# Sixteen of 48 modulation tiles of the first layer: from TensorE sums beside the attention projections to VectorE dot products beside the output projection

## The chip, the core and the metric

The kernel runs on one core of one Trainium2 chip, and nothing else runs on it. The metric is the device time of one execution in microseconds (us). PE is TensorE, PEld its weight loads, DVE VectorE, ACT ScalarE, POOL GpSimd, SP SyncE, which here only issues DMAs. A matmul of four bytes per element is done here as three passes over a rounded high part and a remainder of weight and data, so every weight unit (512 KB) is split on its way: ACT copies its high part (tile `WH`), DVE subtracts it from the raw unit (`WL`).

## What is computed

Two trunks of two layers each run one behind the other. Every layer begins with a vector of modulations, a matrix product of a conditioning vector with a weight of 1024 x 6144; the vector exists for the image (`c`) and for the context (`c_ctx`):

```python
c_act = jax.nn.silu(c); cc_act = jax.nn.silu(c_ctx)
mx = jnp.split(c_act @ ada_w[i] + ada_b[i], 6, axis=-1)
mc = jnp.split(cc_act @ ada_w[i] + ada_b[i], 6, axis=-1)
h_x = modulate(rms_norm(x, norm1_g[i]), mx[0], mx[1])
...
x = x + mx[2] * out_x                       # attention and its output projection
x = x + mx[5] * swiglu(modulate(rms_norm(x, norm2_g[i]), mx[3], mx[4]), ...)
```

The 6144 modulations of a layer are 48 tiles of 128. Tiles 0 to 15 (shift and scale of the first norm) are wanted at once, tiles 16 to 23 (`mx[2]`) at the output projection, tiles 32 to 39 (scale of the second norm) right behind it, tiles 24 to 31 (its shift) with them, and tiles 40 to 47 (`mx[5]`) only in the feed-forward.

## The kernel before

Each engine has its own program, written out by hand, and they meet at semaphores (`on(name, event)` is the value to wait for). Everything of a layer stays in SBUF: 768 columns of tokens (512 image, 256 context), 8 tiles of 128 features.

**Modulations of layer 0.** They are made on TensorE in 12 parts of 512 columns. `ada_sum` (line 761) waits for the two halves of a part (1 MB each, tiles `aV` and `aAR`, issued by SP) and does 16 matmuls of 32 x 512; ACT copies the sum (`ada_copy`, line 1251, `aKF`); `ada_turn` (line 769) turns it by 4 matmuls with a selector, and `ada_finish` adds the bias. (The profile counts a four-byte matmul as more than one record, so a group of four is seen as x8 or x16.) Four parts are made before and in the first norm. The other eight stand one behind each product of the projections of keys and queries: product `u + p`, p from 2 to 9, then the sum of part 4 + QK[p]; its turn stands within the product after it. Beside each product also runs the norm of its head pair: PE sums squares (`square_sum`, line 919), ACT takes the root (line 1256), DVE refines it and turns the pair by its position (`newton` at 1909, then 2372, `stream_shuffle`, sines and cosines). ACT waits within this for `q_normed` (line 2372's result), and the last square sum (of p = 9) stands 18 matmuls into the products for the values (`product_rows`, line 747), where PE waits for `q_squared` of p = 9 and the root of p = 8.

**Modulations of the later layers.** They are made on DVE, in the feed-forward of the layer before: a tile of transposed weights (128 x 1024, 512 KB, `AT`, two buffers, issued by POOL) times the conditioning vector spread over all partitions (`CB`, on which ACT has done Silu, line 1457), with the sum along the row as accumulator (`scalar_tensor_tensor`, line 1895), once for each of the two vectors.

**The output projection.** Eight products `u + n` of 24 x 2 matmuls (line 638; the last two, in `product_tail`, line 682, go by groups, first both over the context, then both over the image). Products alternate between two PSUM tiles, so product n + 2 waits for `x_out` n. On DVE, `project` does for n from 0 to 5: wait for product n, `X += PS * MOD` in two instructions (line 2108), then the low part of the weight of product n + 3 (`refill`, line 1862). Behind n = 1 it does `log_sigmoid`, some twenty small instructions on 8 columns (lines 2732 to 2742). ACT does the high part of the same weight and the square of the new `X` (line 1261), POOL adds the squares up (line 2780: 768 columns, both inputs in SBUF). The second norm begins when the first tail tiles are taken (line 2090). SP issues the weight of unit u + n + 3 as soon as its buffer is free, one queue, in order.

Of the kernel before, what the change touches and what calls it, by code (L numbers as in the profile page):

```python
# [6 lines left out]
ALU = mybir.AluOpType  # L7
# [7 lines left out]
P = 128  # L15
# [15 lines left out]
RING = 6  # L31
Q = 384
NV = 6 * D // P
NA = 6 * D // 512
A0 = 4
EPS = 1e-6
UNIT = KT * P
# [2 lines left out]
U0 = -(S + P)  # L40
NU = L + S - U0
NB = 5 * P + 1
FIRST_PARTS = [0, 2, 1, *range(3, NA)]
FIRST_ADA = (30720, 38912, 49152, 57344, 65536, 73728, 87584, 95776)


# [163 lines left out]
class Memory:  # L210
# [118 lines left out]
    def attention(self):  # L329
        t = self.tile  # L330
        self.aQ = t("aQ", [P, 8, T])
        self.aK = t("aK", [P, 4, 2, T], F32R)
        self.aV = t("aV", [P, 8, L])
        QS0 = t("aQS0", [P, 16, P], F32R)
        top = self.top
        self.aRAW = [t(f"aR{i}", [P, T]) for i in range(2)]
        self.aSQ = t("aSQ", [P, T])
        self.aRI = t("aRI", [P, T])
        self.aT2 = t("aT2", [P, S])
        self.aKF = t("aKF", [P, T])  # L340
        self.aCOS = t("aCOS", [P, S])
        self.aSIN = t("aSIN", [P, S])
        self.aBD = t("aBD", [P, P])
        self.aQG = t("aQG", [P, 2])
        self.aAR = t("aAR", [P, 4, 512])
        self.top = top
        self.aQS = [QS0, t("aQS1", [P, 16, P], F32R)]
        self.aP = [t(f"aP{i}", [P, NB]) for i in range(4)]
        self.aPT = [t(f"aPT{i}", [P, 5 * P]) for i in range(4)]
        self.aID = t("aID", [P, P])  # L350
        self.aMK = t("aMK", [P, 5 * P])
        self.aSK = t("aSK", [P, 16])
        self.aNM = t("aNM", [P, 16])
        self.aRSM = t("aRSM", [P, 16])

    def retention(self):
        t = self.tile
# [264 lines left out]
def tensor_program(PE, M, on, FIRST):  # L622
# [288 lines left out]
    def attention():  # L911
        u = FIRST["qkv"]
        buf = (flat(M.aV, 0, 8).rearrange("p (a n) -> p a n", a=4), M.aAR)

        def square_sum(p):
            PE.wait_ge(*on("q_squared", QK[p]))
            PE.wait_ge(*on("rms", ("q", QK[p - 1])) if p else on("table", "attention"))
            for a, b, _ in ALL:
                mm = PE.matmul(PS[2][:, a:b], M.aBD[:, :], M.aSQ[:, a:b], start=True, stop=True)
            mm.then_inc(*on.up("q_square_sum", QK[p]))  # L920

        def beside(p, at, squares_at, turn_at):

            if at == squares_at and p != 1:
                square_sum(p)
            if at == turn_at and p > 1:
                ada_turn(0, A0 + QK[p], M.aKF)

        product_pair(u, PS, ALL, ("h_lo", "0a", 0), beside_first, amid_first)
        for p in range(2, 10):  # L930
            last = p - 1 if p > 2 else 0
            product(u + p, PS[p % 2], (HH, HL), KT, ALL, ("q_squared", QK[p - 2]), None,
                    lambda k: beside(last, k, 3 if p == 3 else 2, 5))
            if p == 2:
                square_sum(1)
            ada_sum(0, A0 + QK[p], buf, (0, A0 + QK[p] - 1))
        for half in range(2):
            product_rows(u + 10 + half, 4, 4 * half, L, range(6), lambda m: v_place(PS, m), half == 0, half == 1, None, True,
                         (lambda m: ("v_rows", m // 2) if m in (1, 3) else None) if half else None,
                         None if half else lambda at: beside(9, at, 6, 14))  # L940

        PE.wait_ge(*on("aV", 1))
        for step in range(HEADS + LAG + 2):
            i = step
            if i < HEADS:
                b, n = i // 16, i % 16
                kh, ps = M.aK[:, 2 * (n // 8) + n % 2, :, :], PS[n % 2]
                if n == 0:
                    PE.wait_ge(*on("q_stacked", (b, 1)))
                if i == 1:  # L950
                    PE.wait_ge(*on("aV", 2))
                if i > 1:
                    PE.wait_ge(*on("a_max", i - 2))
                for at, k, count in runs(keys(b)):
                    for f in range(2):
                        mm = PE.matmul(ps[:, at * P:(at + count) * P], M.aQS[b % 2][:, n, :], kh[:, f, k * P:(k + count) * P],
                                       start=f == 0, stop=f == 1)
                mm.then_inc(*on.up("a_scores", i))
# [12 lines left out]
            if i >= 0 and i % 2 == 0:
                b, t = i // 16, i % 16 // 2
                out = bank(PS, 6 + t // 4)[:, t % 4 * P:(t % 4 + 1) * P]
                PE.wait_ge(*on("a_turned", i + 1))
                if i == 0:
                    PE.wait_ge(*on("step", ("mod", 0, 2)))
                if t % 4 == 0 and b:
                    PE.wait_ge(*on("o_lo", (b - 1, t // 4)))
                tiles = keys(b)
                for k, kt in enumerate(tiles):  # L980
                    for g in range(2):
                        v0 = (2 * (t // 4) + g) * 64
                        mm = PE.matmul(out[64 * g:64 * g + 64, :], M.aV[:, kt, v0:v0 + 64], M.aPT[(i + g) % 4][:, k * P:(k + 1) * P],
                                       start=(k == 0), stop=(k == len(tiles) - 1))
                mm.then_inc(*on.up("a_values", i // 2))
# [239 lines left out]
def scalar_program(AC, M, on, FIRST, W):  # L1225
# [305 lines left out]
    def attention():  # L1531
# [13 lines left out]
        for p, n in enumerate(QK):  # L1545
# [7 lines left out]
            AC.activation(M.aSQ[:, :], PS[p % 2][:, 0:T], SQUARE).then_inc(*on.up("q_squared", n))  # L1553
            if p:
                refill(u + p + 2)
            if n < 8:
                ada_copy(0, A0 + n, M.aKF[:, 0:512])
            rsqrt(("q", n), M.aRI[:, :], PS[2][:, 0:T], M.aSQ[:, :], ("q_square_sum", n))
            AC.wait_ge(*on("q_normed", n))
            if n in (6, 7):  # L1560
# [290 lines left out]
def vector_program(VE, M, on, FIRST, W):  # L1851
# [14 lines left out]
        ins.then_inc(*on.up("step", event))  # L1866
        VE.wait_ge(*on("step", event))

    def ada_finish(l, part, v0, v1):
        VE.wait_ge(*on("ada_turned", (l, v1 // 4 - 1)))  # L1870
        tr = M.tr.rearrange("p (v j) -> p v j", j=2)
        for j in range(2):
            i = VE.tensor_tensor(MOD[:, l, v0:v1, j], tr[:, v0:v1, j], M.ADB[:, l, v0:v1], ALU.add)
        step(i, ("mod", l, part))
        scales(l, part, v0, v1)

    def scales(l, part, v0, v1):
        for which in range(2):
# [224 lines left out]
    def project(l, segs):  # L2103
        u = FIRST["out", l]
        for n in range(KT - 2):
            VE.wait_ge(*on("product", u + n))
            for a, b, j in segs:
                i = VE.scalar_tensor_tensor(X[:, n, a:b], PS[n % 2][:, a:b], MOD[:, l, 16 + n, j:j + 1], X[:, n, a:b],
                                            ALU.mult, ALU.add)
            i.then_inc(*on.up("x_out", (l, n)))  # L2110
            refill(u + n + 2)
            if l == 0 and n == 1:
                log_sigmoid()

    def turned(l, n):

# [233 lines left out]
    def attention():  # L2350
# [44 lines left out]
        VE.wait_ge(*on("rope", QK[-1]))  # L2395
        for g in range(2):
            stack(0, g)
        ada_finish(0, 2, 4 * A0, NV)
        for v in range(2):
            refill(u + 12 + v)  # L2400
        VE.wait_ge(*on("rope_ctx", QK[-1]))
# [365 lines left out]
def pool_program(PO, M, on, dram):  # L2767
# [15 lines left out]
    def modulation(f, n):  # L2783
# [4 lines left out]
        if n > 1:  # L2788
            PO.wait_ge(*on("ada_taken", order[n - 2]))
        l, v = order[n]  # L2790
        PO.dma_start(M.AT[n % 2][:, :], dram["adat"][l - 1, v]).then_inc(*on.up(f"mod_load{n % 2}", (l, v), 16))  # L2791

    def feed_forward(l):

# [27 lines left out]
    for t, name in ((M.CIN, "cin"), (M.SEL, "sel"), (M.LG, "decay"), (M.ADB, "adb"), (M.GN, "gn"), (M.FG, "finalg"), (M.CW, "ffnconv")):  # L2822
# [2 lines left out]
        src = dram[name]  # L2825
        PO.dma_start(ap, src if len(src.shape) == 2 else src.rearrange("p a b c -> p (a b c)")).then_inc(
            *on.up("c_load" if name in ("cin", "sel") else "small", 0, 16))
    attention()
    PO.wait_ge(*on("o_lo", (5, 1)))
    squares("0b", T)  # L2830
# [23 lines left out]
def sync_program(SP, M, on, FIRST, W, dram, out):  # L2854
# [39 lines left out]
    u = FIRST["qkv"]  # L2894
    buf = (M.aV[:, :, :].rearrange("p (a b) n -> p a (b n)", b=2), M.aAR[:, :, :])
    for n in range(12):
        part = {0: 0}.get(n, n - 2 if 2 < n < 10 else None)
        if part is not None:
            for half in range(2):
                ada(0, A0 + part, half, buf, (0, A0 + part - 1))  # L2900
# [7 lines left out]
    SP.dma_start(M.aID[:, :], dram["ident"]).then_inc(*on.up("aID", 0, 16))  # L2908

    u = FIRST["out", 0]  # L2910
    for n in range(KT):
        load(u + n + 3)
    SP.wait_ge(*on("o_lo", (5, 1)))
    feed_forward(0)

    u = FIRST["ret"]
# [60 lines left out]
def layout(x):  # L2977
# [20 lines left out]
            sel[32 * q + j, j] = 1  # L2998
    d["sel"] = sel
    w = np.concatenate([a["ada_w"], a["w_ada_2"]], 0)  # L3000
    d["ada"] = w[0].reshape(2, 4, P, 12, 512).transpose(3, 0, 2, 1, 4)[FIRST_PARTS].reshape(24, P, 4, 512)
    d["adat"] = w[1:].transpose(0, 2, 1).reshape(3, NV, P, D)
    cb = np.stack([np.stack([a["c"][0], a["c_ctx"]], 0), np.stack([a["c_2"][0], a["c_ctx_2"]], 0)], 0)
    d["cb"] = np.broadcast_to(cb.reshape(2, 1, 2 * D), (2, P, 2 * D))

# [117 lines left out]
```

## Time and profile before

| | |
|---|---|
| Median of 3 runs | 3359.18 us (3356.56 to 3360.82) |
| The profiled execution | 3358.63 us, span of its core 3357.3 us |
| PE busy | 3243.3 us, 97% of the span |
| PE weight loads | 2767.6 us, 82% |
| DVE busy | 2150.5 us, 64% |
| ACT busy | 1389.9 us, 41% |
| POOL busy | 221.0 us, 7% |
| Mean granted PE clock | 0.991 of full speed |
| HBM read | 329.37 MB, 99 GB/s over the span |

The shares are means over stages that differ: in the projections of keys and queries PE has no gap at all, in the attention PE, DVE and ACT take turns, and in the output projection DVE works less than a third of the time. A change that moves work from one stage and engine to another is read from those two stages.

### The profile page before, as it was taken

What the parts mean: (1) busy time and instruction counts of PE and PEld (TensorE: products, weight loads), DVE (VectorE), ACT (ScalarE), POOL (GpSimd) and SP (SyncE); (2) the same over time, 40 slices, a digit from 0 to 9 for tenths busy, and PEclk for the clock granted to TensorE, in tenths of its full rate; (3) what the DMA queues carried; (4) which work ended last, traced back from release to release, by engine and by line L of the source; (5) the groups of instructions that cost most, each with busy time, mean ns of one, the idle gap of its engine ahead of it and who ended that gap; (6) DMA issues with size and microseconds to landing.
All of it is one profiled execution on the core that took longest, in us unless ns stands there. A gap on an engine that the chain in (4) does not pass through costs nothing. (4 is left out here: it accounts for less than half of the span.)

```text
span 3357.3 us, 45065 instructions
## 1 busy us (share of the span) xinstructions
PE 3243.3 (97%) x17830; PEld 2767.6 (82%) x17830; DVE 2150.5 (64%) x3560; ACT 1389.9 (41%) x2242; POOL 221.0 (7%) x336
## 2 busy tenths in 40 slices
PE   7998999999999999999999999999999999999998
PEld 5787789999978888878878886889999987688887
DVE  5678477888665545558788466476777865654444
ACT  5478353333444324342223345353333444542332
POOL 0001100000000000003111000100000010010001
PEclk9999999999999999999999999999999999999999
DMA  6500124444221221226664211113333231122232
GB/s 242 201 23 1 38 74 128 144 132 140 91 93 46 101 78 47 88 76 200 204 200 167 85 45 51 38 67 116 113 104 110 83 103 57 44 88 94 94 101 76
DMA packets 98689, 334.39 MB, mean 100 GB/s; under 512 B 11872, under 2 KB 16768, under 8 KB 95024
## 3 DMA queue, kind: packets, MB, share of 16 engines
q1 hardware_dynamic: 77072, 252.63, 22.4%
q0 software_dynamic: 21408, 78.88, 7.4%
q8 instruction: 142, 2.33, 0.3%
q14 instruction: 67, 0.55, 0.1%
HBM read 329.37 MB, written 2.10 MB: 99 GB/s over the span
## 5 line engine op out<-in xcount | busy, mean ns | idle before, releaser
L1245 ACT ACTIVATE WH<-WR 128x1024 fp32r<-128x1024 f32 (+3 forms) x516 | 443.1, 863 | 916.0 <-PE PS L638 679.5
L1862 DVE TENSOR_TENSOR WL<-WR,WH 128x1024 fp32r<-128x1024 f32 (+3 forms) x516 | 507.9, 986 | 449.1 <-ACT WH L1245 447.9
L638 PE MATMUL PS<-HH,WH 128*128 128x512 f32 x1608 | 544.2, 373 | 8.7 <-DVE WK L2295 3.4
L638 PE MATMUL PS<-HH,WL 128*128 128x512 f32 x1608 | 539.7, 370 | 0.0
L638 PE MATMUL PS<-HL,WH 128*128 128x512 f32 x1608 | 539.2, 369 | 0.0
L638 PE MATMUL PS<-D,WH 128*128 128x512 f32 x1648 | 420.9, 361 | 1.5 <-DVE D L2319 1.4
L638 PEld LDWEIGHTS PS<-HH,WH 128*128 128x128 f32 x1608 | 280.6, 189 | 69.6 <-issue 9.9
L638 PEld LDWEIGHTS PS<-HL,WH 128*128 128x128 f32 x1608 | 279.4, 189 | 52.8 <-issue 1.0
L638 PEld LDWEIGHTS PS<-HH,WL 128*128 128x128 f32 x1608 | 279.7, 189 | 52.2
L638 PEld LDWEIGHTS PS<-D,WH 128*128 128x128 f32 x1648 | 275.7, 188 | 52.6 <-DVE D L2319 3.2
L638 PE MATMUL PS<-D,WL 128*128 128x512 f32 (+1 forms) x824 | 257.3, 360 | 0.0
L2073 DVE SCALAR_TENSOR_TENSOR X<-PS,MOD,X 128x512 f32<-128x512 f32 x198 | 121.2, 644 | 168.7 <-PE PS L638 137.0
L850 PE MATMUL PS<-HH,WH 128*128 128x384 f32 x608 | 204.2, 336 | 4.6 <-DVE WK L2172 4.6
L850 PE MATMUL PS<-HL,WH 128*128 128x384 f32 x608 | 203.7, 335 | 0.0
L850 PE MATMUL PS<-HH,WL 128*128 128x384 f32 x608 | 203.3, 334 | 0.0
L1895 DVE SCALAR_TENSOR_TENSOR AT<-AT,CB 128x1024 f32<-128x1024 f32 x144 | 177.7, 1234 | 8.1 <-ACT CB L1457 6.2
L850 PE MATMUL PS<-XH,WH 128*128 128x384 f32 x456 | 155.1, 340 | 7.3 <-ACT WK L1414 7.3
L638 PEld LDWEIGHTS PS<-D,WL 128*128 128x128 f32 x824 | 138.1, 188 | 25.0
L850 PE MATMUL PS<-XH,WL 128*128 128x384 f32 x456 | 154.5, 339 | 0.0
L850 PE MATMUL PS<-XL,WH 128*128 128x384 f32 x456 | 154.5, 339 | 0.0
L747 PE MATMUL PS<-WH,HH 128*128 128x256 f32 (+1 forms) x416 | 140.5, 338 | 5.1 <-DVE HL L1979 5.1
L2791 POOL DMA_DIRECT2D AT<-in_adat x144 | 76.5, 531 | 995.9 <-DVE AT L1895 980.1
(377 smaller groups left out, 6042.5 us busy)
## 6 DMA issues: line engine op xcount, KB each, us to landing
WR<-in_win SPq DMA_DIRECT2D x176, 512.0 KB, 3.5
AT<-in_adat POOLq DMA_DIRECT2D x144, 512.0 KB, 3.9
WR<-in_wret SPq DMA_DIRECT2D x64, 512.0 KB, 3.7
WR<-in_zin SPq DMA_DIRECT2D x36, 512.0 KB, 3.5
WR<-in_wdn SPq DMA_DIRECT2D x32, 448.0 KB, 3.4
WR<-in_wdn SPq DMA_DIRECT2D x48, 256.0 KB, 2.7
WR<-in_wdn SPq DMA_DIRECT2D x32, 320.0 KB, 3.0
AR<-in_ada SPq DMA_DIRECT2D x8, 1024.0 KB, 19.1
```

Source lines behind the costliest of these rows:

```text
L638: mm = PE.matmul(dst[:, a:b], w(u)[:, k * P:(k + 1) * P], h[:, k, a:b], start=(k == 0 and i == 0), stop=(k == nk - 1 and i == 2))
L747: mm = PE.matmul(dst(m), h[:, k0 + k, m * P:(m + 1) * P], w(u)[:, k * width:(k + 1) * width], start=(first and k == 0 and i == 0 and not ( ...
L850: mm = PE.matmul(dst, w(key)[:, k * P:(k + 1) * P], h[:, k, :], start=(k == 0 and n == 0 and i in (1, 2, 7)), stop=(k == 3 and n == 2), sk ...
L1245: AC.activation(M.hi(u), M.raw(u), COPY).then_inc(*on.up("w_hi", u))
L1862: VE.tensor_tensor(M.lo(u), M.raw(u), M.hi(u).bitcast(F32), ALU.subtract).then_inc(*on.up("w_lo", u))
L1895: i = VE.scalar_tensor_tensor((AT if j == len(cols) - 1 else PS[3])[:, :], AT[:, :], 1.0, M.CB[:, j, :], ALU.mult, ALU.mult, accum_out=MOD ...
L2073: i = VE.scalar_tensor_tensor(X[:, m, a:b], src[:, a:b], MOD[:, l, 40 + m, j:j + 1], X[:, m, a:b], ALU.mult, ALU.add)
L2791: PO.dma_start(M.AT[n % 2][:, :], dram["adat"][l - 1, v]).then_inc(*on.up(f"mod_load{n % 2}", (l, v), 16))
```

## The change

It takes tiles 24 to 31 and 40 to 47 of layer 0 from TensorE. The parts shrink from 12 to 8 (`NA` = 8), so the sums and turns behind products 6, 7, 8 and 9 go, with their loads and copies. The 16 tiles are made as in later layers, by `first_dots` on DVE: before it waits for product n of the output projection it makes 3 tiles for n = 0 to 3 and 2 for n = 4 and 5 (`FIRST_AT`), each with two dot products of 128 x 1024 against a new tile `CB0` (1 MB, loaded by POOL's queue in the first norm; ACT does Silu on it at p = 8, between the copies of the pair and the root). SP loads the tiles into `AT`, two buffers, in its queue of weights; tile i waits until tile i - 2 is taken. None can be loaded before the attention ends, as `AT` lies where the attention's tiles are, and SP now waits there (`o_lo`) after one weight where it had issued those it could. A sum with the bias (`first_bias`) follows behind n = 5.

```diff
-NA = 6 * D // 512
+FIRST_PARTS = [0, 2, 1, 3, 4, 5, 8, 9]
+FIRST_DOTS = [*range(24, 32), *range(40, 48)]
+FIRST_AT = (0, 3, 6, 9, 12, 14, 16, 16, 16)
+NA = len(FIRST_PARTS)
...
+        self.aDT = t("aDT", [P, D])
+        self.top = top
...
+        self.CB0 = t("CB0", [P, 2, D])
...
-            if at == turn_at and p > 1:
+            if at == turn_at and p > 1 and A0 + QK[p] < NA:
                 ada_turn(0, A0 + QK[p], M.aKF)
...
-            ada_sum(0, A0 + QK[p], buf, (0, A0 + QK[p] - 1))
+            if A0 + QK[p] < NA:
+                ada_sum(0, A0 + QK[p], buf, (0, A0 + QK[p] - 1))
...
-            if n < 8:
+            if A0 + n < NA:
                 ada_copy(0, A0 + n, M.aKF[:, 0:512])
+            if p == 8:
+                AC.wait_ge(*on("cb_load", 0))
+                AC.activation(M.CB0[:, :, :], M.CB0[:, :, :], ACT.Silu).then_inc(*on.up("cb", 0))
             rsqrt(("q", n), M.aRI[:, :], PS[2][:, 0:T], M.aSQ[:, :], ("q_square_sum", n))
...
+    def first_dots(at):
+
+        for n in range(FIRST_AT[at], FIRST_AT[at + 1]):
+            v = FIRST_DOTS[n]
+            if n == 0:
+                VE.wait_ge(*on("cb", 0))
+            VE.wait_ge(*on(f"ada_load{6 + n % 2}", ("dot", v)))
+            if n:
+                VE.wait_ge(*on("ada_taken", (0, FIRST_DOTS[n - 1])))
+            for j in range(2):
+                i = VE.scalar_tensor_tensor((M.AT[n % 2] if j else M.aDT)[:, :], M.AT[n % 2][:, :], 1.0, M.CB0[:, j, :],
+                                            ALU.mult, ALU.mult, accum_out=MOD[:, 0, v, j:j + 1])
+            i.then_inc(*on.up("ada_taken", (0, v)))
+
+    def first_bias():
+        VE.wait_ge(*on("ada_taken", (0, FIRST_DOTS[-1])))
+        for v0, v1 in ((24, 32), (40, 48)):
+            for j in range(2):
+                i = VE.tensor_tensor(MOD[:, 0, v0:v1, j], MOD[:, 0, v0:v1, j], M.ADB[:, 0, v0:v1], ALU.add)
+        step(i, ("mod", 0, 3))
...
         for n in range(KT - 2):
+            if l == 0:
+                first_dots(n)
             VE.wait_ge(*on("product", u + n))
...
+            if l == 0 and n == KT - 3:
+                first_bias()
...
+    PO.wait_ge(*on("ada_sum", (0, A0 - 1, 1)))
+    PO.dma_start(flat(M.CB0, 0, 2), dram["cb"][0]).then_inc(*on.up("cb_load", 0, 16))
...
     u = FIRST["out", 0]
+    load(u + 3)
+    SP.wait_ge(*on("o_lo", (5, 1)))
     for n in range(KT):
-        load(u + n + 3)
-    SP.wait_ge(*on("o_lo", (5, 1)))
+        if n:
+            load(u + n + 3)
+        for i, v in list(enumerate(FIRST_DOTS))[FIRST_AT[n]:FIRST_AT[n + 1]]:
+            if i > 1:
+                SP.wait_ge(*on("ada_taken", (0, FIRST_DOTS[i - 2])))
+            SP.dma_start(M.AT[i % 2][:, :], dram["adat"][0, v]).then_inc(*on.up(f"ada_load{6 + i % 2}", ("dot", v), 16))
```

## Rows read from the trace of the kernel before

**Rows 1.** Stages: us, busy time per engine, PE clock, DMA share, GB/s.
```profile
94.86:145.49 50.63, 50.63 (x305) 37.60 (x304) 36.20 (x53) 26.82 (x41) 0.00 (x0) 1.00 0.55 208
...
353.15:405.66 52.51, 52.51 (x288) 45.53 (x289) 17.10 (x37) 9.56 (x10) 10.53 (x6) 0.97 0.17 51
```

**Rows 2.** Timeline of PE, projections of queries: start, us, line, tile, count.
```profile
145.05 0.51 PE L638 MATMUL PS<-HH,WL 128*128 128x512 f32 x2
...
145.49 1.06 PE L761 MATMUL PS<-aV,CAC 128*32 128x512 f32 x8
...
147.34 0.62 PE L638 MATMUL PS<-HH,WH 128*128 128x512 f32 x2
...
154.03 0.95 PE L769 MATMUL PS<-SEL,aKF 128*128 128x2 f32 x8
...
154.84 0.59 PE L638 MATMUL PS<-HH,WH 128*128 128x512 f32 x2
...
158.13 1.07 PE L761 MATMUL PS<-aV,CAC 128*32 128x512 f32 x8
...
162.24 1.02 PE L919 MATMUL PS<-aSQ,aBD 128*128 128x512 f32 x2
```

**Rows 3.** Timeline of ACT, the same stretch.
```profile
147.00 1.06 ACT L1245 ACTIVATE WH<-WR 128x1024 fp32r<-128x1024 f32 x1
...
151.05 0.90 ACT L1256 ACTIVATE aRI<-PS,EPSC 128x768 f32<-128x768 f32 x1 [2.51 <-PE PS L919]
```

**Rows 4.** Instructions of line 1457: ns min/median/max, first and last start.
```profile
L1457 ACT ACTIVATE CB<-CB x2: 1919/1919/1919, 496.5 to 2262.6; 128x2048 f32<-128x2048 f32 x2
```

**Rows 5.** Timeline of ACT behind the output projection.
```profile
412.57 1.28 ACT L1256 ACT_TABLE_LOAD   x1
```

**Rows 6.** Timeline of DVE, projections of queries and values.
```profile
152.87 0.96 DVE L1909 SCALAR_TENSOR_TENSOR aSQ<-PS,aSQ 128x768 f32<-128x768 f32 x1 [3.55 <-ACT aSQ L1258]
...
154.85 1.02 DVE L2372 SCALAR_TENSOR_TENSOR aR<-aR,aQG,aRI 128x768 f32<-128x768 f32 x1
...
180.85 1.23 DVE L1862 TENSOR_TENSOR WL<-WR,WH 128x1024 fp32r<-128x1024 f32 x1 [3.94 <-ACT WH L1245]
```

**Rows 7.** Instructions of line 1895, the dot products of later layers.
```profile
L1895 DVE SCALAR_TENSOR_TENSOR AT<-AT,CB x144: 1210/1219/1749, 498.5 to 2668.6; 128x1024 f32<-128x1024 f32 x144
```

**Rows 8.** Timeline of DVE, the output projection.
```profile
363.47 1.14 DVE L2108 SCALAR_TENSOR_TENSOR X<-PS,MOD,X 128x512 f32<-128x512 f32 x2 [10.37 <-PE PS L638]
...
364.62 1.23 DVE L1862 TENSOR_TENSOR WL<-WR,WH 128x1024 fp32r<-128x1024 f32 x1
...
374.24 1.82 DVE L2732 TENSOR_SCALAR MOD<-MOD 128x8 f32<-128x8 f32 x1
...
380.50 1.14 DVE L2108 SCALAR_TENSOR_TENSOR X<-PS,MOD,X 128x512 f32<-128x512 f32 x2
...
408.74 0.48 DVE L2090 SCALAR_TENSOR_TENSOR X<-PS,MOD,X 128x256 f32<-128x256 f32 x1 [0.50 <-PE PS L682]
```

**Rows 9.** DMA issues of the output projection's weights: count, KB, us to landing.
```profile
WR<-in_wo SPq DMA_DIRECT2D x8, 512.0 KB, 3.8
```

**Rows 10.** Timeline of POOL, the output projection.
```profile
365.58 1.97 POOL L2780 TENSOR_TENSOR WK<-WK,WK 128x768 f32<-128x768 f32 x1 [11.68 <-ACT WK L1261]
...
374.05 1.98 POOL L2780 TENSOR_TENSOR WK<-WK,WK 128x768 f32<-128x768 f32 x1 [6.50 <-ACT WK L1261]
```

**Rows 11.** Timeline of DVE, dot products beside POOL.
```profile
1544.34 1.65 DVE L1895 SCALAR_TENSOR_TENSOR PS<-AT,CB 128x1024 f32<-128x1024 f32 x1
```

**Rows 12.** Timeline of POOL, the same stretch.
```profile
1544.15 0.74 POOL L2809 TENSOR_TENSOR WK<-X 128x256 f32<-128x256 f32 x1
```

**Rows 13.** Timeline of PE after a wait in the feed-forward.
```profile
504.38 0.66 PE L850 MATMUL PS<-XH,WH 128*128 128x384 f32 x1 [3.81 <-ACT WK L1414]
```

**Rows 14.** Stage behind that wait; columns as in rows 1.
```profile
504.38:507.40 3.02, 3.02 (x10) 3.02 (x10) 2.68 (x6) 2.34 (x5) 0.00 (x0) 0.50 0.82 283
```

More of the change, by code:

```diff
@@ L42 @@
 NB = 5 * P + 1
-FIRST_PARTS = [0, 2, 1, *range(3, NA)]
 FIRST_ADA = (30720, 38912, 49152, 57344, 65536, 73728, 87584, 95776)
@@ L1867, in step, with ada_finish @@
         VE.wait_ge(*on("step", event))
-    def ada_finish(l, part, v0, v1):
-        VE.wait_ge(*on("ada_turned", (l, v1 // 4 - 1)))
+    def ada_finish(l, part, pieces):
+        VE.wait_ge(*on("ada_turned", (l, NA - 1)))
         tr = M.tr.rearrange("p (v j) -> p v j", j=2)
-        for j in range(2):
-            i = VE.tensor_tensor(MOD[:, l, v0:v1, j], tr[:, v0:v1, j], M.ADB[:, l, v0:v1], ALU.add)
+        for v0, v1 in pieces:
+            for j in range(2):
+                i = VE.tensor_tensor(MOD[:, l, v0:v1, j], tr[:, v0:v1, j], M.ADB[:, l, v0:v1], ALU.add)
         step(i, ("mod", l, part))
-        scales(l, part, v0, v1)
+        scales(l, part, pieces[0][0], pieces[-1][1])
+    def first_dots(at):
[13 more added lines that the diff above has]
+        for v0, v1 in ((24, 32), (40, 48)):
+            for j in range(2):
+                i = VE.tensor_tensor(MOD[:, 0, v0:v1, j], MOD[:, 0, v0:v1, j], M.ADB[:, 0, v0:v1], ALU.add)
+        step(i, ("mod", 0, 3))
     def scales(l, part, v0, v1):
@@ L2397, in attention @@
             stack(0, g)
-        ada_finish(0, 2, 4 * A0, NV)
+        ada_finish(0, 2, ((16, 24), (32, 40)))
         for v in range(2):
@@ L2790, in modulation @@
         l, v = order[n]
[L2791 removed]
+        PO.dma_start(M.AT[n % 2][:, :], dram["adat"][l, v]).then_inc(*on.up(f"mod_load{n % 2}", (l, v), 16))
     def feed_forward(l):
@@ L2896, in sync_program @@
     for n in range(12):
-        part = {0: 0}.get(n, n - 2 if 2 < n < 10 else None)
+        part = {0: 0}.get(n, n - 2 if 2 < n < 3 + NA - A0 - 1 else None)
         if part is not None:
@@ L3000, in layout @@
     w = np.concatenate([a["ada_w"], a["w_ada_2"]], 0)
-    d["ada"] = w[0].reshape(2, 4, P, 12, 512).transpose(3, 0, 2, 1, 4)[FIRST_PARTS].reshape(24, P, 4, 512)
-    d["adat"] = w[1:].transpose(0, 2, 1).reshape(3, NV, P, D)
+    d["ada"] = w[0].reshape(2, 4, P, 12, 512).transpose(3, 0, 2, 1, 4)[FIRST_PARTS].reshape(2 * NA, P, 4, 512)
+    d["adat"] = w.transpose(0, 2, 1).reshape(4, NV, P, D)
     cb = np.stack([np.stack([a["c"][0], a["c_ctx"]], 0), np.stack([a["c_2"][0], a["c_ctx_2"]], 0)], 0)
```

## The prediction

> **What bounds the kernel.** I read first the table of stages, for the two stages the change touches. Between 94.86 and 145.49 us, four periods of the query projections, PE is busy for all of the 50.63 us at full clock; between 353.15 and 405.66, the first six products of the output projection, again for all of the 52.51, while DVE works 17.10 [rows 1]. In both stages the end is set by the sum of what PE does; in the second DVE has 35 us free. Then I read the timelines of PE, ACT and DVE of one period of the first stage, for what leaves it and what waits behind it, and those of DVE and POOL in the second, for what fits into it. The chain of waits, followed back from the end, does not reach these stages and says nothing here.
>
> **What is removed.** One period of PE, from sum to sum, is 158.13 - 145.49 = 12.64 us. The 16 matmuls of a sum stand between the last pair of a product (145.05 plus the 0.35 that pairs are apart) and the next product at 147.34: 1.94. The turn takes 154.84 - 154.03 = 0.81. Each new start costs some 0.08 more, so a sum with its turn is worth 2.9, and a period without them 9.74 [rows 2]. Four go: 11.6 us. Loads of 2 MB a period and the copy by ACT were hidden and are worth nothing. Is there another chain that keeps the period at 12.6? ACT starts the root of p = 8 at 151.05, 5.65 after the product's end at 145.40, because the square sum stands behind the modulation sum [rows 3]; it moves up by 1.94. DVE starts the refinement 1.82 later and is done with the pair some 6 us after that, which is 11.3 after the product's end; the next pair's root then starts at 9.74 + 3.7. DVE and ACT stay ahead by about a microsecond, and the period follows PE.
>
> **What is added there.** The Silu of `CB0` on ACT at p = 8. It has 2048 columns, 1.92 us [rows 4], and changes the table before and after it, 1.28 each [rows 5]: 4.48 us. The refill of ACT ends at 147.95 [rows 3], so the root starts at 152.5 in place of 149.1. The result for which ACT waits next (line 2372) ends 154.85 + 1.02 = 155.87, that is 4.8 after the start of the root [rows 6]: now 157.3. Behind it ACT copies 0.4, and only then takes the raw copy and the square of p = 9, 1.5 together: 159.2. PE comes to that square sum 2.25 into the products for the values (162.24 against 158.13 + 1.86) [rows 2], which is 145.40 + 9.74 + 2.25 = 157.4. It waits 1.8 us. Before the attention DVE stood idle for 3.94 us until these products were done [rows 6]; its pair of p = 9 now ends later against them by about a microsecond, which that idle time covers. The load of `CB0` meets only loads of parts and weights that are wanted later. Gain of this stage: 11.6 - 1.8 = 9.8 us; at most 11.6 (no wait), at least 8 (if the chain of DVE holds the three short periods up by 0.6 each).
>
> **What is added in the output projection.** I count DVE's time from the start of product 0 (353.15). The dots are 32 at 1.22 each with little overlap [rows 7]: 2.4 us a tile, 38.4 in all; 2.3 if they overlap fully, 2.5 with the wait for the tile before. An update of `X` with its refill takes from 363.47 to 365.8: 2.3, and `log_sigmoid` from 374.24 to the next update at 380.50: 6.2 [rows 8]. Four more costs:
>
> First, tile 0 can't be loaded before the attention ends. The nearest row is a unit of the same 512 KB on the same queue, 3.8 us from issue to landing [rows 9], with 0.2 for the semaphore 4.0.
>
> Second, with two buffers tile i is issued when tile i - 2 is taken, and the dots of tile i - 1 (2.4) cover only part of 3.8 + 0.3. In each group of three the third tile waits 1.6 us; the first two have the update, or more, as cover. Four groups: 6.4. For groups of two nothing.
>
> Third, POOL. Its square sum starts 0.97 after an update is done (365.58 against 363.47 + 1.14), waits for the end of the refill and runs 1.78 to 367.55 [rows 8, 10]. Today nothing follows the refill but an idle stretch. The one exception is `log_sigmoid`: its first instruction on 8 columns takes 1.82 us and ends 376.06, as POOL's sum does at 376.03 [rows 8, 10]. A dot beside a short POOL instruction until 1544.89 started at 1544.34 and took 1.65, not 1.22 [rows 11, 12]: held for 0.4, then run at its own speed. Now a dot stands behind the refill for n = 0, 2, 3 and 4, and is held about 1.6 each time: 6.4. If instead the two shared the bandwidth, the dot would take 1.35 times as long (1.65 / 1.22) for 1.9 us: 0.5 each, 2.0 in all. The 1.82 is nearest to the first reading, and I take it.
>
> The Trainium skill bears on this (SBUF — State Buffer, Who interferes with whom): DVE with two inputs in SBUF and a GpSimd instruction that reads SBUF exclude each other for the whole instruction, and the one issued second waits. By that rule the four holds are 6.4, by the sharing that I weighed it against 2.0; the trace agrees with the rule on the 1.82 us, and update instructions with one input in PSUM would not be held.
>
> Fourth, SP's queue: the weights of n = 1 to 5 now stand between tiles. Each lands many microseconds before ACT wants it; nothing.
>
> The sum until the update of n = 5 is done: 4.0 + 38.4 + 6.4 + 6.4 + five updates with refill 11.5 + 6.2 + the last update 1.1 = 74.0 us. PE was there at 408.74 - 0.2 - 353.15 = 55.4: the second tail tile needs that update, and the first tail tile over the context was then done [rows 8]. So PE falls back 18.6. It does so in pieces: product 4 waits for the update of n = 2, which ends near 43.5 where PE is free at 35.6; product 5 waits for n = 3, near 56 against 52; the second tail tile waits near 6 us. All of them lie in DVE's one sequence, so the first waits don't add to the last.
>
> Then the tail. The bias (four small adds and a semaphore, 0.7) is held by POOL's sum of n = 5, 1.6, and stands ahead of the first tail tile's update. The mean of the context is then ready about 1 us late for PE. Or, PE's clock: after a wait of 3.81 us its next matmuls of 384 columns took 0.66 and on [rows 13], with the granted clock at 0.50 for 3.0 us, 1.2 in place of 2.4 GHz [rows 14]; it lost 1.4 us. Behind a wait of 6 us I expect the same. The two overlap: 1.0 us for both together, at most 2.5. The clock that falls in product 4 is absorbed, as PE waits for DVE again behind it. Loss of this stage: 19.6 us; at least 12.6 (third cost at 2.0, tail at nothing, tiles at 2.3), at most 25 (landings of 5 us, tiles of 2.5).
>
> What follows, the second norm and the feed-forward, is the same work and moves as a whole. Net: 19.6 - 9.8 = +9.8, against the profiled 3358.63 us: 3368.4. That execution lies 0.55 under the median of the three; a measured median would be 3369. I take 3368.5 us.
>
> **The rivals.** All times against 3358.6. Less than 0.2% (6.7 us) can hardly be told from no change, so the bounds are 3351.9 and 3365.3.
>
> *The port is shared, not locked, and the tail hides its wait.* Loss 19.6 - 4.4 - 1.0 = 14.2, net +4.4: 3363.0, no difference. For it: POOL's instruction lengths vary, and some of a hold may fall into a wait for a tile. Against it: the 1.82 us for 8 columns.
>
> *The other side: the free 35 us of DVE are enough.* With no waits for tiles, no holds and tiles of 2.3, the sum is 59.6, the loss 4.2, and with the whole 11.6 of the first stage the kernel is 7.4 faster: 3351.2. The mechanism is a tile's cost, its waits included: to pass 0.2% it must be under 2.23 us where the gain is 9.8 (the loss may be 3.1, so DVE's sequence 58.5, less 22.8 for all that is not a tile, by 16), and under 2.34 where it is 11.6. The dots alone take 2.3 to 2.4. What speaks for it is only the busy share of DVE.
>
> *Landings are slow.* SP's queue has weights between the tiles; if a tile behind a weight lands after 6 us and not 3.8, each of the four waits and the first grow by 2.2: +11, net +20: 3379. For it: two transfers share the engines. Against: the two need only a small share of the DMA engines in this stage (0.17 now, under 0.5 then).
>
> *The first stage keeps its period*, because the norm chain of ACT and DVE sets it: gain 3 in place of 9.8, 3375. Against it: PE has no gap at all there and waits for neither.
>
> **Chances.** The forecast 0.56, ports shared or milder 0.25, DVE has room 0.04, slow landings 0.09, first stage keeps its period 0.06. So faster 0.04, same 0.27 (the second case, and little of the forecast's lower edge), slower 0.69. The forecast alone spans 3365 to 3373 (tile 2.3 to 2.5, 1.5 for landings, 1.5 for the clock). The range for 8 in 10 takes in most of the milder case and the upper edge: 3362 to 3375.
>
> **What the profile would show.** Right: periods of 9.7 us behind product 6, a PE wait near 1.8 in the products for the values, DVE without a gap from 357 on (all less 9.8) but for four waits for DMA of 1.6; a dot of 2.8 us behind the refills of n = 0, 2, 3 and 4; PE waits of about 8, 3 and 6 us, named DVE `X`. Wrong: dots of 1.65 there (shared), the wait of products 4 and 5 missing (DVE has room), waits for DMA of 4 (slow landings), or periods still over 11.

## The result, and the profile after

The changed kernel took 3367.22 us (median of 8 runs, 3365.36 to 3371.38), the kernel before 3356.39 us beside it (8 runs, 3353.96 to 3360.82). The ratio is 1.0031, with a 95% interval of 1.0021 to 1.0040: 7 to 13 us slower (10.8 by the medians), where 9.8 was forecast, and inside the range of 3362 to 3375. The profiled execution took 3365.97 us, with a span of 3364.5.

The page's busy times show where work went: PE 9.6 us less than before, DVE 45.9 more.

```profile
PE 3233.7 (96%) x17734; PEld 2764.5 (82%) x17734; DVE 2196.4 (65%) x3630; ACT 1391.8 (41%) x2241; POOL 221.2 (7%) x337
```

**First stage.** The timeline of ACT after the change, at p = 8:

```profile
139.72 0.81 ACT L1556 ACTIVATE aR<-PS 128x768 f32<-128x768 f32 x1 [1.09 <-PE PS L643]
140.43 0.81 ACT L1559 ACTIVATE aSQ<-PS 128x768 f32<-128x768 f32 x1
141.12 1.06 ACT L1251 ACTIVATE WH<-WR 128x1024 fp32r<-128x1024 f32 x1
142.20 1.28 ACT L1566 ACT_TABLE_LOAD   x1
143.49 1.92 ACT L1566 ACTIVATE CB<-CB 128x2048 f32<-128x2048 f32 x1
145.43 1.28 ACT L1262 ACT_TABLE_LOAD   x1
146.72 0.90 ACT L1262 ACTIVATE aRI<-PS,EPSC 128x768 f32<-128x768 f32 x1
```

The Silu and its two table loads stand between the refill (ends 142.18) and the root (146.72): 4.5 us. The raw copy before this one starts at 129.95, so a period without a sum is 9.77 us, against 12.64 [rows 2]. In PE's timeline the price of the Silu is one wait, in the products for the values:

```profile
151.33 0.28 PE L752 MATMUL PS<-WH,HL 128*128 128x256 f32 x1
153.44 1.56 PE L924 MATMUL PS<-aSQ,aBD 128*128 128x512 f32 x4 [1.83 <-ACT aSQ L1559]
```

From the first square sum of the queries to the first scores of the attention, 123.98 us became 114.50: 9.5 gained. The attention behind it takes the same time (171.31 before, 171.43 after).

**Output projection.** DVE's timeline after the change: the three tiles before the update of n = 0, what stands behind the refills of n = 0, 1 and 4, and the end:

```profile
347.31 1.23 DVE L1897 SCALAR_TENSOR_TENSOR aDT<-AT,CB 128x1024 f32<-128x1024 f32 x1 [3.65 <-DMA AT<-in_adat]
348.46 1.22 DVE L1897 SCALAR_TENSOR_TENSOR AT<-AT,CB 128x1024 f32<-128x1024 f32 x1
...
349.79 1.23 DVE L1897 SCALAR_TENSOR_TENSOR aDT<-AT,CB 128x1024 f32<-128x1024 f32 x1
...
353.08 1.23 DVE L1897 SCALAR_TENSOR_TENSOR aDT<-AT,CB 128x1024 f32<-128x1024 f32 x1 [0.91 <-DMA AT<-in_adat]
...
355.37 1.14 DVE L2141 SCALAR_TENSOR_TENSOR X<-PS,MOD,X 128x512 f32<-128x512 f32 x2
356.43 1.22 DVE L1871 TENSOR_TENSOR WL<-WR,WH 128x1024 fp32r<-128x1024 f32 x1
357.56 2.88 DVE L1897 SCALAR_TENSOR_TENSOR aDT<-AT,CB 128x1024 f32<-128x1024 f32 x1
...
369.65 1.82 DVE L2767 TENSOR_SCALAR MOD<-MOD 128x8 f32<-128x8 f32 x1
...
406.88 2.88 DVE L1897 SCALAR_TENSOR_TENSOR aDT<-AT,CB 128x1024 f32<-128x1024 f32 x1
...
413.31 1.14 DVE L2141 SCALAR_TENSOR_TENSOR X<-PS,MOD,X 128x512 f32<-128x512 f32 x2
...
415.50 2.03 DVE L1905 TENSOR_TENSOR MOD<-MOD,ADB 128x8 f32<-128x8 f32 x4
```

Two tiles of a group start 2.48 apart (347.31, 349.79). The third waits 0.91 for its transfer (1.09, 1.02 and 1.12 in the next groups). The dot behind a refill takes 2.88 and not 1.22, and the small adds of the bias take 2.03. POOL's timeline beside it:

```profile
357.48 1.87 POOL L2815 TENSOR_TENSOR WK<-WK,WK 128x768 f32<-128x768 f32 x1 [13.03 <-ACT WK L1267]
...
406.79 1.89 POOL L2815 TENSOR_TENSOR WK<-WK,WK 128x768 f32<-128x768 f32 x1 [6.74 <-ACT WK L1267]
415.40 1.87 POOL L2815 TENSOR_TENSOR WK<-WK,WK 128x768 f32<-128x768 f32 x1 [6.73 <-ACT WK L1267]
```

POOL's sum ends at 359.35 and the dot that started at 357.56 at 360.44, 1.1 later: it stood until POOL was done and then ran at its own speed. PE's timeline shows where it waits for the updates:

```profile
385.27 0.98 PE L643 MATMUL PS<-HH,WH 128*128 128x512 f32 x2 [6.56 <-DVE X L2141]
397.36 0.58 PE L643 MATMUL PS<-HH,WH 128*128 128x512 f32 x2 [0.69 <-DVE X L2141]
414.60 0.55 PE L687 MATMUL PS<-HH,WH 128*128 128x256 f32 x1 [5.51 <-DVE X L2141]
```

Behind the first and the last of these waits PE works at half its clock. The windows of these stretches after the change (granted clock third from the end):

```profile
385.27:391.00 5.73, 5.73 (x18) 4.87 (x19) 5.63 (x6) 1.68 (x2) 1.87 (x1) 0.50 0.26 87
414.60:418.80 4.20, 4.20 (x20) 4.20 (x21) 3.41 (x6) 1.15 (x2) 2.09 (x2) 0.53 0.36 127
```

The stage by windows, first before and then after: from product 0 to the second tail tile, and from there to the first product of the feed-forward.

```profile
353.15:408.55 55.40, 55.40 (x313) 48.42 (x314) 19.46 (x40) 11.47 (x12) 11.11 (x7) 0.97 0.16 48
408.55:445.57 37.02, 33.79 (x178) 27.95 (x176) 25.22 (x43) 21.24 (x37) 3.42 (x3) 1.00 0.09 29
```
```profile
343.71:414.60 70.89, 58.13 (x313) 50.41 (x313) 61.78 (x104) 10.40 (x12) 10.11 (x6) 0.89 0.49 171
414.60:453.43 38.83, 35.57 (x176) 29.74 (x176) 28.15 (x48) 21.98 (x38) 3.89 (x3) 0.95 0.08 28
```

DVE works 61.78 of 70.89 us, where it worked 19.46 of 55.40: it has become the bound. The stage lost 15.5 us, and the norm behind it 1.8: 17.3. The 1.8 is PE's clock: behind the second tail tile PE is busy for 35.57 us in place of 33.79, and its gaps are the same (3.26 and 3.23). The bias, which POOL holds for 1.65 us, shows in no gap of PE. Less the 9.5 of the first stage that is 7.8 us by landmarks (starts of chosen instructions, the same in every profile), and the two profiled spans differ by 7.2. How far a profile can be trusted here: the start-up before the first square sum of the queries ended anywhere from 57.7 to 59.8 us in the eleven profiles of this study.

### The profile page after: what moved, and what is told of

Same layout as the page of the kernel before. It is cut to its first block and busy times, and to the rows that moved or that the text cites. A ratio compares the mean times of both kernels' runs of the same rounds, so it can differ in the third digit from the quotient of the medians.

```text
span 3364.5 us, 44958 instructions
## 1 busy us (share of the span) xinstructions
PE 3233.7 (96%) x17734; PEld 2764.5 (82%) x17734; DVE 2196.4 (65%) x3630; ACT 1391.8 (41%) x2241; POOL 221.2 (7%) x337
```

## The experiments

Times below are medians in us; a ratio is against the kernel before, in runs beside the kernel's own. There it took 3357.67 (30 runs) beside the first stage alone, the short sums, the four buffers and the later Silu, 3357.93 (19) beside the row in PSUM and the last three kernels, and 3356.67 (15) beside the later logarithm. Three landmarks are read from each profile: first square sum of the queries to first scores (123.98 before, 114.50 after), product 0 to the end of the update of n = 5 (53.86, 70.74), and product 0 to the feed-forward's first product (92.42, 109.72).

### first_stage_alone: what the first stage gives by itself

The four sums stay away, and the 16 tiles are made nowhere (only the bias is left of them).

```diff
-            if l == 0:
-                first_dots(n)
...
-        for i, v in list(enumerate(FIRST_DOTS))[FIRST_AT[n]:FIRST_AT[n + 1]]:
...
-            SP.dma_start(M.AT[i % 2][:, :], dram["adat"][0, v])
```

> The changed kernel without its dot products and without the loads of their tiles (the sixteen tiles are left out, only a bias is written); the sums on TensorE are gone and the Silu on ScalarE stays. It measures the gain of the first stage by itself. My theory: the output projection starts 9.4 us earlier, as in the profile of the changed kernel, nothing is lost behind it, and the kernel is 9.4 us faster than before (ratio 0.9972). Rival, that the work removed from TensorE was partly hidden and the 9.4 us are given back elsewhere: 3 us or less. Rival, that the loss of the change lies in later stages and not in the output projection: then it is still slower than before.

Measured: 3347.21 (3344.70 to 3351.52), ratio 0.9971 (0.9961 to 0.9982). Landmarks 114.50, 53.86 and 92.43: the first is that of the changed kernel, the other two those of the kernel before to 0.01 us. So the change is the sum of two independent parts, and the first is worth 9.5 us with its Silu in place.

### short_pool_sums: POOL's sums made short

The sum of squares of n = 0 to 5 goes over 8 columns in place of 768; most of that sum is left out.

```diff
+            if tag == "0b" and b - a == n:
+                b = a + 8
```

> The changed kernel, with the six sums of squares that GpSimd does beside the output projection cut from 768 columns to 8 (most of these sums of squares is left out). It tests whether the dot products that took 2.9 us are held by GpSimd. Port held for a whole instruction: the four dots behind the refills take 1.3 in place of 2.9 us, the first instruction of the logarithm 0.2 in place of 1.8, the bias loses 1.6 too; VectorE's sequence to the last update shrinks by 8.2 us from 70.7 to about 62.5, the second tail tile waits not at all or 1 us, and the kernel is 7 to 9 us faster than the changed one, about 2 to 3 above the one before less: ratio to before near 1.0005. Bandwidth shared: the dots take 1.2 to 1.5 and the gain is near 2 us. If the 2.9 us come from something else (the DMA that writes the next tile): unchanged, ratio 1.003.

Measured: 3357.16 (3355.43 to 3361.26), ratio 1.0002 (0.9993 to 1.0010). The update of n = 5 ends at 62.40, 8.3 earlier: five holds of 1.65, four of dots and one of `log_sigmoid`. The timeline of DVE in this kernel, behind the refills of n = 0 and 1:

```profile
358.56 1.22 DVE L1897 SCALAR_TENSOR_TENSOR aDT<-AT,CB 128x1024 f32<-128x1024 f32 x1
...
368.94 0.17 DVE L2767 TENSOR_SCALAR MOD<-MOD 128x8 f32<-128x8 f32 x1
```

The dot is back at 1.22, and the instruction on 8 columns at 0.17 from 1.82 [rows 8]. The holds come from POOL's instruction. The feed-forward starts at 99.65, 10.1 earlier, so 1.7 more came from behind the update: PE's last wait is 2.51 us in place of 5.51, and PE works at full clock behind it:

```profile
407.10:411.30 4.20, 4.20 (x30) 3.98 (x31) 2.27 (x7) 1.68 (x4) 0.96 (x2) 1.00 0.34 127
```

The bias takes 0.40 us in place of 2.03, but PE's gaps from there to the feed-forward are as long as with the hold (3.27 and 3.26 us).

### row_in_psum: is it an exclusion over two inputs in SBUF?

POOL's sum stays whole. The first conditioning row lies in PSUM, so the first dot of a tile has one input in SBUF, the second dot still two.

```diff
+            AC.activation(PS[3][:, :], M.CB0[:, 0, :], COPY)
...
-                i = VE.scalar_tensor_tensor(..., M.AT[n % 2][:, :], 1.0, M.CB0[:, j, :],
+                i = VE.scalar_tensor_tensor(..., M.AT[n % 2][:, :], 1.0, M.CB0[:, 1, :] if j else PS[3][:, :],
```

> The changed kernel, with the first of the two conditioning rows copied by ACT into a PSUM tile that is free in this stage; the first dot of every tile reads it from there, the second still reads both inputs from SBUF. If an instruction of DVE with two inputs in SBUF is excluded by POOL's sum of squares, the first dot behind a refill is no longer held (2.87 us becomes about 1.2), and the second dot, which starts 1.2 later, is held only for what is left of POOL's 1.87, about 0.5: the update of n = 5 ends some 4 x 1.15 = 4.6 us earlier, near 66 us behind the start of product 0 in place of 70.7, and the time is 4 to 5.5 us less than the changed kernel's, ratio to the kernel before near 1.0018. If the dot behind the refill is long for another reason (it waits for its own tile, for the refill, for the accumulator, or SBUF's bandwidth is shared), it stays at 2.9 or near it and nothing changes: ratio 1.003.

Measured: 3361.26 (3356.68 to 3364.23), ratio 1.0010 (1.0001 to 1.0018). DVE behind the refill of n = 0, and the third tile of the next group:

```profile
358.45 1.22 DVE L1901 SCALAR_TENSOR_TENSOR aDT<-AT,PS 128x1024 f32<-128x1024 f32 x1
...
359.59 1.73 DVE L1901 SCALAR_TENSOR_TENSOR AT<-AT,CB 128x1024 f32<-128x1024 f32 x1
...
366.56 1.22 DVE L1901 SCALAR_TENSOR_TENSOR aDT<-AT,PS 128x1024 f32<-128x1024 f32 x1 [2.74 <-DMA AT<-in_adat]
```

```profile
358.38 1.87 POOL L2819 TENSOR_TENSOR WK<-WK,WK 128x768 f32<-128x768 f32 x1 [13.03 <-ACT WK L1267]
```

The first dot runs through under POOL's sum at full speed, and so does POOL; the second, with two inputs in SBUF, stands from 359.59 until POOL is done at 360.25. That is the exclusion, dot by dot, in one tile and beside one POOL instruction, and no sharing of bandwidth. The update of n = 5 ended 3.1 us earlier, not 4.6: four holds fell from 1.65 to 0.5 as expected, but one of the waits for a transfer grew from 1.09 to 2.74. That tile landed 5.2 us after the tile whose buffer it takes was done, where it took 3.5 in the changed kernel. Why is not settled: in both kernels a unit of weight was issued 0.4 us behind this tile.

### four_buffers: the waits for tiles

The two halves of `CB` (free in this stage) serve as third and fourth buffer.

```diff
-            VE.wait_ge(*on(f"ada_load{6 + n % 2}", ("dot", v)))
+            AT = M.A4[n % 4]
+            VE.wait_ge(*on(f"ada_load{4 + n % 4}", ("dot", v)))
...
-            if i > 1:
-                SP.wait_ge(*on("ada_taken", (0, FIRST_DOTS[i - 2])))
+            if i > 3:
+                SP.wait_ge(*on("ada_taken", (0, FIRST_DOTS[i - 4])))
```

> The changed kernel with four buffers for the tiles in place of two (the two more lie where the later conditioning rows will be), each tile issued when the one four before it is taken. My theory: the four waits for a DMA of 0.9 to 1.1 us go, VectorE's sequence shrinks from 70.7 to 66.6 us, the kernel is 4 us faster than the changed one (5 if TensorE's clock does not fall in the then shorter last wait); ratio to before 1.002. Rival, that TensorE's falling clock is the larger part of the loss: it falls as before and the gain is below 2 us.

Measured: 3363.05 (3360.84 to 3365.01), ratio 1.0016 (1.0008 to 1.0025). The four waits are gone and only the first landing stays (3.69). The update of n = 5 ends at 67.07, 3.7 earlier; the four waits measured 0.91 + 1.09 + 1.02 + 1.12 = 4.1 in the changed kernel. In the waits of PE for `X` 12.8 us have become 9.3.

### silu_later: the Silu out of the pair's chain

The Silu moves from p = 8 to between ACT's last two refills of this stage, ahead of its copies of the values, where ACT has slack.

```diff
-            if p == 8:
-                AC.wait_ge(*on("cb_load", 0))
-                AC.activation(M.CB0[:, :, :], M.CB0[:, :, :], ACT.Silu)
...
+            if v == 0:
+                AC.wait_ge(*on("cb_load", 0))
+                AC.activation(M.CB0[:, :, :], M.CB0[:, :, :], ACT.Silu)
```

> The changed kernel with the Silu of the conditioning rows moved from the eighth pair of the projections to behind the first of the last two refills of this stage, where ScalarE stood idle for 4.3 us before the attention. My theory: TensorE's wait of 1.8 us in the products for the values goes, the Silu and its table (3.2 us) fit into the idle time, and the output projection starts 1.8 us earlier: 1.8 us faster than the changed kernel. Rival: the chain of the norms or the weights' refill then ends later than TensorE, and the gain is 0 to 0.5 us.

Measured: 3363.00 (3359.55 to 3364.82), ratio 1.0015 (1.0007 to 1.0024). PE's wait of 1.83 is gone and the first landmark is 112.40, 2.1 shorter (1.8 expected). Against 123.98 the four sums are thus worth 11.6, the forecast's 4 x 2.9.

### log_later: is all of DVE's sequence on the path?

`log_sigmoid`, hidden under PE in the kernel before, moves to the last products of the feed-forward.

```diff
-            if l == 0 and n == 1:
-                log_sigmoid()
...
+                if l == 0 and ch == LAST[0] and m == 2:
+                    log_sigmoid()
```

> The changed kernel with one edit: log_sigmoid, which stands in DVE's program behind the update of n = 1, is moved to the last products of the feed-forward of the same layer. Its 6.2 us were hidden under PE in the kernel before. If DVE's one sequence sets the end of the output projection, all of them are on the path now; without them the next dot stands behind the refill and is the fifth that POOL holds, by 1.65: the update of n = 5 ends 6.2 - 1.65 = 4.5 us earlier, near 66.2 us behind the start of product 0, and the time is 4 to 5 us under the changed kernel's, ratio to the kernel before near 1.0018. If instead the last tiles' transfers or PE's own falls of clock set the end, it stays near 70 and the ratio near 1.003.

Measured: 3362.01 (3359.22 to 3364.52), ratio 1.0016 (1.0007 to 1.0025). The update of n = 5 ends at 66.90, 3.8 earlier. One wait for a transfer is longer, and a fifth dot is held, behind the refill of n = 1:

```profile
367.96 1.23 DVE L1897 SCALAR_TENSOR_TENSOR aDT<-AT,CB 128x1024 f32<-128x1024 f32 x1 [1.85 <-DMA AT<-in_adat]
...
371.31 1.21 DVE L1871 TENSOR_TENSOR WL<-WR,WH 128x1024 fp32r<-128x1024 f32 x1
372.45 2.88 DVE L1897 SCALAR_TENSOR_TENSOR aDT<-AT,CB 128x1024 f32<-128x1024 f32 x1
```

That wait was 1.09 in the changed kernel; the 0.8 is what is missing from the 4.5, within 0.1. Work that cost nothing in the kernel before costs its length less the hold that it had absorbed.

### Eight, twelve and sixteen tiles

Three kernels join the findings: the Silu later, four buffers, and all tiles that are not dots stay sums on TensorE. With eight (tiles 24 to 31) `log_sigmoid` stays and both rows are in SBUF; with twelve (40 to 43 as well) and sixteen the first row is in PSUM and `log_sigmoid` is moved. With eight and twelve the bias stands before the update of n = 5.

```diff
-FIRST_PARTS = [0, 2, 1, 3, 4, 5, 8, 9]
-FIRST_DOTS = [*range(24, 32), *range(40, 48)]
-FIRST_AT = (0, 3, 6, 9, 12, 14, 16, 16, 16)
+FIRST_PARTS = [0, 2, 1, 3, 4, 5, 8, 9, 11]
+FIRST_DOTS = [*range(24, 32), *range(40, 44)]
+FIRST_AT = (0, 3, 5, 7, 9, 11, 12, 12, 12)
```

> Half of the tiles: 24 to 31 as dots on DVE (2 for n = 0, 2 for n = 1, none for n = 2, 2, 1 and 1), tiles 40 to 47 stay sums on TensorE (10 parts of 512 columns, not 8). With it the Silu between the root and the copies of the next pair, four buffers for the tiles (the two small ones and the two halves of the large one), and the bias behind the dots of n = 5. My account: DVE's sequence is 3.6 + 8 x 2.45 + five updates 11.5 + log_sigmoid 6.2 + holds of at most 3 x 1.65 + 1.8 = 48 us and less than PE's 55.4, so the output projection loses nothing, update of n = 5 done at 54 behind product 0 as before; the first stage gains 2 x 2.9 = 5.8: ratio 0.9983. If the loss is not the length of DVE's sequence but something each dot does to PE (SBUF or DMA contention, the clock), about half of the loss stays, 8 us: ratio 1.0006.

> Three quarters of the tiles: 24 to 31 and 40 to 43 as dots on DVE, 44 to 47 on TensorE (9 parts of 512 columns). As the kernel with eight, and the first conditioning row read from PSUM, and log_sigmoid moved out of the output projection into the last products of the feed-forward of the layer. My account: DVE's sequence 3.6 + 12 x 2.45 + 11.5 + 1.1 + 4 x 0.5 + 1.5 = 49 and less than PE's 55.4: no loss, gain 3 x 2.9 = 8.7, ratio 0.9974. If log_sigmoid costs in its new place what it costs in the old, or DVE falls behind at one product, some 3 us less gain: ratio 0.9983.

> All 16 tiles as in the change, with everything found so far: Silu later, four buffers, the first row from PSUM, log_sigmoid moved to the feed-forward. My account: DVE's sequence 3.6 + 16 x 2.45 + 11.5 + 1.1 + 4 x 0.5 + bias 0.7 = 58 against PE's 55.4, so the update of n = 5 is done near 57 to 58 behind product 0 and PE waits some 3 to 4 us, 1 more by the clock; gain 11.6, net -7 to -8: ratio 0.9978. So twelve and sixteen should be nearly equal. If each tile costs more than 2.45 (2.6 with semaphores and landings), the loss is 6 and the ratio 0.9985.

| | median (runs) | ratio, 95% | to the scores | to x of n = 5 | to the feed-forward |
|---|---|---|---|---|---|
| before | 3357.93 (19) | | 123.98 | 53.86 | 92.42 |
| eight | 3348.89 (7) | 0.9974 (0.9963 to 0.9985) | 118.16 | 53.02 | 91.51 |
| twelve | 3346.25 (5) | 0.9962 (0.9949 to 0.9974) | 115.24 | 52.40 | 90.90 |
| sixteen | 3350.23 (7) | 0.9972 (0.9961 to 0.9983) | 112.39 | 56.88 | 95.64 |

The first column of landmarks falls by 5.8, 8.7 and 11.6: 2.9 for each sum that goes. In the output projection eight and twelve cost nothing. The window of the twelve over that stage and the start of the norm shows PE without a gap at full clock, with DVE at 53.89 of 69.32:

```profile
344.23:413.55 69.32, 69.32 (x395) 60.53 (x396) 53.89 (x89) 19.76 (x27) 14.40 (x9) 1.00 0.43 152
```

and DVE waits for PE again before the updates of n = 3, 4 and 5, the last by 2.96 us:

```profile
395.49 1.14 DVE L2149 SCALAR_TENSOR_TENSOR X<-PS,MOD,X 128x512 f32<-128x512 f32 x2 [2.96 <-PE PS L644]
```

With sixteen DVE never waits for PE from the first tile to the update of n = 5, and PE waits once:

```profile
PE PS L688 <- DVE X L2147: 2.4, 1, 2.4
```

Against the kernel before it gives back 3.2 us of its 11.6: PE waits, and the clock falls once more behind the wait:

```profile
399.19:403.39 4.20, 4.20 (x24) 4.20 (x25) 3.42 (x6) 1.15 (x2) 2.08 (x2) 0.65 0.36 125
```

All three kernels are faster than the kernel before. The medians of eight and twelve lie 9.0 and 11.7 us under it, the landmarks give 6.7 and 10.3; both are inside the intervals. Of the 6.7 and 10.3, 0.9 and 1.5 come from the output projection, which was meant to stay as it was. The 1.5 of the twelve is PE's clock in the first 4 us of product 0, here in the kernel before and with twelve:

```profile
353.15:357.15 4.00, 4.00 (x15) 3.43 (x16) 0.00 (x0) 0.00 (x0) 0.74 (x1) 0.61 0.03 6
```
```profile
344.23:348.23 4.00, 4.00 (x23) 3.49 (x24) 0.45 (x1) 1.00 (x1) 0.74 (x1) 1.00 0.74 257
```

Full clock at this place is seen in two of the eleven profiles (twelve, and the Silu later), and no run ties it to the change; the others, sixteen with them, have 0.57 to 0.61. The 0.9 of the eight is a product of 8.32 us in place of 8.48 (pairs of matmuls 0.347 apart on average, not 0.353), for a reason that stays open. Without these two the landmarks give 5.8 for eight, 8.7 for twelve and 11.6 - 3.2 = 8.4 for sixteen. So twelve has the lowest median, but its interval overlaps those of the other two, and the landmarks don't set it apart from sixteen either: the last four tiles gain 2.9 in the first stage and lose 3.2 behind it.

## Why the prediction was right, step by step

**First stage: right.** Sum and turn worth 2.9: measured 2.9 three times over (eight, twelve and sixteen, all with the Silu later). Periods of 9.74: 9.77. The wait behind the Silu 1.8: 1.83; taking it away gave 2.1. Gain 9.8: 9.5.

**DVE sets the output projection: right.** The forecast's sum was 74.0 us to the end of the update of n = 5, measured 70.7. Term by term, all from the timeline after the change:

| term | forecast | measured |
|---|---|---|
| first tile's landing | 4.0 | 3.6 |
| 16 tiles | 38.4 | 38.2 |
| waits for the third tile, x4 | 6.4 | 4.1 |
| dots held by POOL, x4 | 6.4 | 6.6 |
| five updates with refill | 11.5 | 11.0 |
| `log_sigmoid` | 6.2 | 6.2 |
| last update | 1.1 | 1.1 |

(Measured tiles: 2.48 + 2.38 + 2.29 for each of four groups of three and 2.48 + 2.30 for each of two groups of two, holds and waits taken out; the hold is 2.88 - 1.22.)

**The term that was mis-sized most** is the wait for the third tile: 1.0 each in place of 1.6, 2.3 of the 3.3 us by which the sum was too large. The forecast took 3.8 us for a landing and 0.3 for semaphores [rows 9] against a cover of 2.4. The issues of DMAs after the change, count, KB and median us to landing:

```profile
AT<-in_adat SPq DMA_DIRECT2D x14, 512.0 KB, 3.5
```

3.5 less a tile's 2.48 is the 1.0 that was measured. The kernel with four buffers shows that the term is real: without it 3.7 us are gone.

**The holds, where the rival stood, are settled.** The sharing that would have given 0.5 each is out: a dot with one input in PSUM runs at full speed beside the same POOL instruction, the next one with two in SBUF stands still until it ends, and a short POOL instruction takes all five holds away. The price was 1.65 us a time. The forecast weighed a rule of the Trainium skill (SBUF — State Buffer, Who interferes with whom): two inputs in SBUF contend with a GpSimd instruction that reads SBUF, and the loser waits for the whole instruction. The held dots agree. The same section says that an instruction with at most one input in SBUF and outside the 2-port modes does not contend, and the 1.22 us dot beside POOL's 1.87 agrees. The row by which the forecast chose, the 1.82 us on 8 columns, is not an instruction with two inputs in SBUF: it has one. That section counts this operation (`tensor_scalar`) among those that can enter a 2-port mode and so can contend; no run here tested which mode it ran in. So that row showed that POOL can hold DVE for a whole instruction; that a dot is held as long came from the rule and not from the row.

**PE's waits** were forecast near 8, 3 and 6 us (4 for the second in the working, 56 against 52) and came to 6.6, 0.7 and 5.5. The first is smaller, as the update of n = 2 was done 41.4 us behind the start of product 0 (385.12 - 343.71) and not 43.5. The second is smaller as the update of n = 3 was done at 53.5 and not 56, and as product 4, at half clock for its first part, took 11.4 us (385.27 to 396.67), where one at full clock takes 8.3. The forecast named this absorption and did not take it off its 3 or 4 us.

**The tail** was taken as 1.0 for the held bias and the clock together, 2.5 at most, and cost 1.8. The bias was held as expected (2.03 against 0.40 with the short sums). But PE's busy time behind the second tail tile is 1.8 longer and its gaps are not, which puts all of it on the clock: 4.2 us at a granted clock of 0.53, where [rows 14] had 3.0 at 0.50. No run has the held bias with full clock behind it, so the split is read from PE's timeline and not tried by itself.

**The upper bound** of the loss, 25 us, does not come out of its own terms: landings of 5 us make the first landing and four waits 1.2 longer each, 6.0, and tiles of 2.5 another 1.6, together 27. The measured loss was far below either. The refill of ACT that was read as ending at 147.95 ends at 148.06 by [rows 3], which changes the wait by 0.1.

**The sum.** 19.6 - 9.8 = 9.8 was forecast; the landmarks give 17.3 - 9.5 = 7.8, and the two medians differ by 10.8 (interval 7.0 to 13.4). The landmarks compare the two profiled executions, and these lie 2.2 us above their median before (3358.63 against 3356.39) and 1.3 below it after (3365.97 against 3367.22). That is the 3 us between the two figures; which of them is nearer to the true effect the runs do not settle. In the six kernels of single experiments the difference of the medians and that of the landmarks agree to 1.8 us. So the closeness of 3368.5 to the measured 3367.22 is partly luck: by landmarks the forecast loss was 2.3 us too large (a sequence of DVE 3.3 too long, a tail 0.8 too short, and rounding) and the gain 0.3 too large.

## What to carry to other kernels

An engine that is busy a third of a stage offers its idle time only as far as its whole sequence, with waits for buffers, holds and small work that used to be hidden, stays shorter than the bound engine's: here 16 tiles of 2.4 us of work cost 3.1 each with four waits of 1.0 and four holds of 1.65, and they made 6 us of `log_sigmoid` visible. So move as many pieces as the sequence holds, not all: with the waits and holds mended, eight or twelve of the tiles cost nothing in the output projection, and the last four of sixteen cost what they had gained. Before stacking two-input DVE work behind a POOL instruction, put one operand in PSUM or order the work so that POOL runs beside something else, and place a piece with table loads (4.5 us of ACT) where the engine behind it has slack.

## What the runs showed of the hardware

- A DVE instruction of 8 columns with one input in SBUF (`TENSOR_SCALAR`, 0.17 us by itself) is held for all of POOL's sum as well: 1.82. The hold of this tiny instruction was as long as that of a dot (1.65 us). With POOL's sum short it took 0.17 again.
- POOL's sum of 768 columns took 1.87 to 1.89 us whether a dot was held behind it or one with PSUM input ran beside it. In that pairing neither slowed the other.
- Behind a wait of 6.56 us PE worked 5.7 us at a granted clock of 0.50 (1.2 in place of 2.4 GHz), behind one of 5.51 it was 4.2 us at 0.53, behind the 3.81 us of [rows 13] 3.0 at 0.50. Behind a wait of 2.40 (sixteen tiles) the next 4.2 us had 0.65, behind one of 2.51 (short sums) 1.00: the same length of wait was followed by a tail 1.6 us longer than before in one kernel and 0.1 in the other. In this chain only the last wait paid for its stretch in full, because the half clock behind the first (11.4 us for product 4) shortened the next wait for DVE to 0.69.
- A tile of 512 KB landed 3.5 us after its issue (the median), but once after 5.2 in the kernel with the row in PSUM, and once after 5.1 in the changed kernel itself (issued between 384 and 396 us, where no wait for a tile grew by it). A model with one landing time can't give this.
